# Experts of a routed layer in 12 fixed rounds of four 32-token groups, instead of tiles of 128 rows of one expert each

## The chip, the core and the metric

The kernel runs on one core of a Trainium2 chip. The metric is the device time of one execution in microseconds (us); all inputs and outputs are float32 in HBM. Besides that time there is a profile of one execution, with times from the first to the last instruction of the program (its span). TensorE's matrix work is called PE, its loading of the stationary operand PEld, VectorE DVE, ScalarE ACT, GpSimd POOL, and the engine that issues most transfers SP.

## The reference

One layer of a diffusion backbone for 128 context tokens and 512 latent tokens (640 in all, width 1024): modulation, a projection, attention beside an RWKV-7 scan, an output projection, and then a mixture of experts. Only the last part is touched by the change:

```python
def hier_moe(h, lp):
    x = h.reshape(B * T, D)
    lc = x @ router_c + router_c_b;  g_idx = argmax(lc)                  # 1 of 4 groups
    lf_sel = (x @ router_f + router_f_b) of the chosen group             # 4 experts
    top_w, top_i = lax.top_k(softmax(lf_sel), 2);  top_w /= sum(top_w)   # 2 of 4 experts
    for e in range(16):
        hid = silu(x @ exp_gate[e]) * (x @ exp_up[e])                    # 1024 -> 512
        out = out + combine[:, e:e+1] * (hid @ exp_down[e])              # 512 -> 1024
```

Each of the 640 tokens goes to two experts, so 1280 rows are computed. The weights of one expert are three matrices of 2 MB (gate, up, down). For the inputs that the kernel is run with, the routing of the reference gives the experts 0 to 15 these numbers of rows: 92, 108, 58, 72, 60, 110, 137, 69, 86, 59, 70, 59, 98, 49, 108, 45.

## The kernel before

The program is a row of blocks; at the end of a block all engines wait for each other. The earlier blocks (modulation, projection, attention, scan) take some 570 us and are not changed but for one store and a table of constants. The block from line 1753 on does the output projection, the second norm and the routing. POOL scatters each token's row to the region of its two experts in a scratch tensor in HBM (`xg_d`, 640 rows for each expert; line 1777, two batches, of 3 and of 2 token tiles). DVE counts the rows of each expert and writes a table (lines 2088 to 2106): for each tile of 128 rows its expert and its first row, and how many pairs of tiles there are. An expert with up to 128 rows has one tile, one with 137 has two. The block from line 2143 on works through that table in a loop with a number of turns known only at run time, two tiles to a turn, after a first tile (expert 0) that stands ahead of the loop. For tile i:

- SP loads the weights of the tile's expert into one of two places, `wg`, `wu`, `wd`, with gate and up when the tile before has finished its up product (`u6_mm`) and down when the down product of the tile two before has ended (`y6_mm`). It also loads the tile's 128 token rows (`load_x`).
- PE turns the 128 rows (`x_turn`, 8 turnings of 128x128, line 2178), multiplies them by gate and up (line 2186, 16 products of 128 rows by 512 columns), turns the hidden values (`h_turn`, line 2192) and multiplies by down (line 2200, 8 products). The order in the loop is turn of the hidden values of i-1, gate and up of i, turn of the rows of i+1, down of i-1.
- ACT and DVE take the results out of PSUM (lines 2232 to 2245, 2277 to 2285), and ACT stores the tile's 128 output rows (line 2248) in `yg_d`.

The weights are read as `"(k p) n -> p k n"`: partition p gets the matrix rows p, 128+p, 256+p and so on, in stretches of 2 KB each (gate, up) or 4 KB each (down). PE reads a turning's source as 128 neighbouring columns.

SP has loaded the weights of expert 0 in the block before: up at its start (line 1763), gate when the last tile's concatenation is done (1765), down when the output projection is done (1767). No other expert is known before the table is written.

The last block (line 2305) gathers for each token its two output rows, by indices in `back_i`, weighs and adds them, and stores the outputs.

## Time and profile before

| | us |
|---|---|
| median of 3 runs | 1112.93 |
| lowest and highest run | 1109.16, 1114.7 |
| span of the profiled execution | 1107.9 |
| expert block, first to last PE instruction | 688.7 to 1073.4 |
| one tile of an expert on PE, steady | 21.94 |

The page gives the profiled execution by its span alone; what lies around the span, before the first and after the last instruction, is not shown. The span is 5.0 us under the median of the runs. A line of the trace that shows a group of instructions gives the start of the first, the time from there to the end of the last, the engine, the line of the kernel, and in brackets how long the engine had been idle before and who released it. Each float32 product shows as two MATMUL records.

### The profile page before, as it was taken

What the parts mean: (1) busy time and instruction counts of PE and PEld (TensorE: products, weight loads), DVE (VectorE), ACT (ScalarE), POOL (GpSimd) and SP (SyncE); (2) the same over time, 40 slices, a digit from 0 to 9 for tenths busy, and PEclk for the clock granted to TensorE, in tenths of its full rate; (3) what the DMA queues carried; (4) which work ended last, traced back from release to release, by engine and by line L of the source; (5) the groups of instructions that cost most, each with busy time, mean ns of one, the idle gap of its engine ahead of it and who ended that gap; (6) DMA issues with size and microseconds to landing.
All of it is one profiled execution on the core that took longest, in us unless ns stands there. A gap on an engine that the chain in (4) does not pass through costs nothing. (4 is left out here: it accounts for less than half of the span.)

```text
span 1107.9 us, 18535 instructions
## 1 busy us (share of the span) xinstructions
PE 970.2 (88%) x7858; PEld 575.7 (52%) x7858; DVE 424.7 (38%) x783; ACT 274.8 (25%) x522; POOL 81.4 (7%) x133
## 2 busy tenths in 40 slices
PE   4899999979778778999979982999999999999960
PEld 1465555536456568899954552444444444444420
DVE  2323642233388876687756554000000000000006
ACT  2221222223676622233230120111111111111112
POOL 0600000010000020122200003000000000000002
PEclk9999999998699966999989985999999999999995
DMA  9904342538999510133246226969899899989717
GB/s 332 306 9 152 124 168 89 191 120 352 407 404 403 219 50 8 45 81 96 70 130 243 77 76 247 365 230 333 314 347 346 318 329 347 345 310 337 281 40 282
DMA packets 98629, 247.18 MB, mean 223 GB/s; under 512 B 7540, under 2 KB 12564, under 8 KB 98304
## 3 DMA queue, kind: packets, MB, share of 16 engines
q1 hardware_dynamic: 87104, 219.91, 54.7%
q0 software_dynamic: 5632, 13.97, 4.1%
q10 hardware_dynamic: 5824, 12.28, 2.8%
q8 instruction: 55, 0.90, 0.3%
q14 instruction: 14, 0.11, 0.0%
HBM read 176.51 MB, written 67.01 MB: 220 GB/s over the span
## 5 line engine op out<-in xcount | busy, mean ns | idle before, releaser
L2186 PE MATMUL ps<-arena 128*128 128x512 f32 x544 | 238.9, 596 | 1.7 <-ACT arena L2236 1.7
L2186 PEld LDWEIGHTS ps<-arena 128*128 128x128 f32 x544 | 102.4, 191 | 126.3 <-issue 125.6
L2200 PE MATMUL ps<-arena 128*128 128x512 f32 x272 | 121.2, 598 | 3.6 <-ACT arena L2240 3.6
L711 PE MATMUL ps<-arena 128*128 128x512 f32 (+3 forms) x448 | 123.6, 435 | 0.0
L711 PEld LDWEIGHTS ps<-arena 128*128 128x128 f32 (+1 forms) x448 | 67.7, 188 | 60.2 <-issue 59.3
L2200 PEld LDWEIGHTS ps<-arena 128*128 128x128 f32 x272 | 50.7, 191 | 61.9 <-issue 61.9
L1855 PE MATMUL ps<-arena 128*128 128x512 f32 x160 | 72.4, 606 | 1.9 <-PEq L1324 1.9
L2277 DVE TENSOR_TENSOR arena<-arena,ps 128x512 f32<-128x512 f32 x17 | 11.7, 689 | 136.0 <-ACT arena L2232 136.0
L578 DVE SCALAR_TENSOR_TENSOR arena<-arena 128x128 f32<-128x128 f32 (+3 forms) x56 | 30.9, 552 | 82.6 <-ACT arena L447 81.1
L2285 DVE COPY arena<-ps 128x512 f32<-128x512 f32 x17 | 11.8, 692 | 125.7 <-PE ps L2200 125.7
L644 PE MATMUL ps<-arena 128*128 128x512 f32 (+1 forms) x160 | 52.6, 485 | 1.1 <-ACT arena L405 1.1
L2236 ACT ACTIVATE arena<-ps 128x1024 f32<-128x1024 f32 x18 | 18.5, 1026 | 140.2 <-PE ps L2178 140.2
L1855 PEld LDWEIGHTS ps<-arena 128*128 128x128 f32 x160 | 30.3, 194 | 36.9 <-issue 36.9
L2280 DVE TENSOR_TENSOR arena<-arena,ps 128x512 f32<-128x512 f32 x17 | 11.7, 689 | 94.6 <-PE ps L2186 94.6
L956 PE MATMUL ps<-arena 128*128 128x128 f32 x160 | 26.0, 297 | 22.9 <-DVE arena L1180 19.5
L615 PE MATMUL ps<-arena 128*32 128x512 f32 x192 | 28.6, 635 | 15.7 <-DMA arena<-in_w_mod_dram 15.7
L644 PEld LDWEIGHTS ps<-arena 128*128 128x128 f32 x160 | 29.8, 189 | 20.8 <-issue 17.4
L1366 POOL DMA_DIRECT2D arena<-arena x40 | 20.5, 519 | 258.8 <-issue 155.7
L2310 POOL DMA_INDIRECT arena<-expert_outputs,back_i x10 | 9.8, 984 | 401.0 <-PEq L2305 398.2
L2245 ACT ACTIVATE arena<-ps 128x512 f32<-128x512 f32 x17 | 10.2, 598 | 103.0 <-PE ps L2200 103.0
L1174 DVE TENSOR_REDUCE arena<-ps 128x1 f32<-128x640 f32 x32 | 24.9, 820 | 26.9 <-PE ps L936 26.9
L956 PEld LDWEIGHTS ps<-arena 128*128 128x128 f32 x160 | 18.1, 148 | 29.1 <-DVE arena L1180 23.1
(311 smaller groups left out, 1342.9 us busy)
## 6 DMA issues: line engine op xcount, KB each, us to landing
gathered_tokens<-arena SPq DMA_DIRECT2D x16, 2560.0 KB, 27.0
arena<-in_exp_up_dram SPq DMA_DIRECT2D x17, 2048.0 KB, 18.0
arena<-in_exp_gate_dram SPq DMA_DIRECT2D x17, 2048.0 KB, 13.0
arena<-in_exp_down_dram SPq DMA_DIRECT2D x17, 2048.0 KB, 9.9
arena<-in_w_mod_dram SPq DMA_DIRECT2D x12, 2048.0 KB, 12.4
arena<-gathered_tokens SPq DMA_DIRECT2D x18, 512.0 KB, 15.3
expert_outputs<-arena ACTq DMA_DIRECT2D x17, 512.0 KB, 8.1
arena<-in_w_in_dram SPq DMA_DIRECT2D x4, 2048.0 KB, 8.6
```

What stands on the lines that cost most here:

```text
L578: ins = dve.scalar_tensor_tensor(o[:, a:b], r_[:, base + off:base + off + b - a], mu[0:m, k, e:e + 1], o[:, a:b], ALU.mult, ALU.add)
L615: mm = pe.matmul(ps[32 * g:32 * g + 32, bank, :], cond32[:, k, :], ring[:, slot_of(what), k, :], start=(k < 4), stop=(k >= 4))
L644: mm = pe.matmul(ps[:, b + half, 0:w], hT[:, k, tt * P:(tt + 1) * P], ring[:, slot_of(("qkv", half)), k, 0:w], start=(k == 0), stop=(k == ...
L711: mm = pe.matmul(ps[0:m, b, 0:hi - lo], ring[:, slot_of(what), k, (e % 4) * P:(e % 4) * P + m], hT[:, k, lo:hi], start=(k == 0), stop=(k = ...
L956: mm = pe.transpose(ps[:, 4 + y // 4, (y % 4) * P:(y % 4 + 1) * P], prob[:, g, y * P:(y + 1) * P], ident)
L1174: dve.tensor_reduce(negmax[:, n:n + 1], score_banks(g), AX.X, ALU.max, negate=True).then_inc(max_ok, 1)
L1366: pool.dma_start(rows(u, 1 - z)[:, z, p * NC4:(p + 1) * NC4], rows(vt, p)[:, chunk_at(z, s)]).then_inc(ld_v[s % 2], 16)
L1855: mm = pe.matmul(ps[:, b, :], catT[k4][:, j, tt * P:(tt + 1) * P], wout[:, half, NC4 * k4 + j, :], start=(k4 == 0 and j == 0), stop=(k4 == ...
L2186: mm = pe.matmul(ps[:, b, :], xgT[:, k, :], w[u][:, k, :], start=(k == 0), stop=(k == KT - 1))
L2200: mm = pe.matmul(ps[:, Y0 + half, :], hidT[:, k, :], wd[u][:, k, half * 512:(half + 1) * 512], start=(k == 0), stop=(k == 3))
L2236: act.activation(xgT, ps[:, XT0:XT0 + 2, :].rearrange("p b (k t) -> p (b k) t", t=P), ACT.Copy).then_inc(xgT_ok, 1)
L2285: dve.tensor_copy(yo[:, u, 512:], ps[:, Y0 + 1, :]).then_inc(yo_v, 1)
```

## The change

The experts are taken in a fixed number of 12 rounds, each of 128 columns of tokens in four groups of 32. There are 16 places for experts in a fixed order; place n has a capacity of `CAPQ[n]` groups of 32 rows (48 groups in all), and `RANK_OF[n]` says the expert of which rank in the order of counts stands there (0 for the fullest). Expert 0 always has the first place, of 96 rows. A round can hold the end of one expert's places and the start of the next: five rounds (1, 2, 4, 8, 10) have one expert, four (3, 6, 9, 11) have two experts with 64 rows each, three (0, 5, 7) have two with 96 and 32 rows. In a round with two experts PE makes each product in two pieces of 64 or four pieces of 32 stationary columns, each with the weights of its own expert as the moving operand and its own PSUM partitions. Rows over a place's capacity would go through a loop after the rounds, one tile of 128 at a time; the counts above all fit.

```diff
-NT = 25
-MIN_TILES = NE
+QROWS = 32
+CAPQ = (3, 5, 4, 2, 2, 4, 3, 3, 3, 3, 4, 2, 2, 4, 2, 2)
+RANK_OF = (15, 0, 1, 9, 10, 2, 5, 6, 7, 8, 3, 11, 12, 4, 13, 14)
+NR = sum(CAPQ) // 4
+NOV = 12
...
-        wg = [view(WG0, KT, FE), view(CB, KT, FE)]
...
+        wg = [view(RING + j * PIECE, KT, FE) for j in (8, 7, 6)]
+        wu = [view(RING + j * PIECE, KT, FE) for j in (4, 5, 3)]
+        wd = [view(RING + j * PIECE, 4, D) for j in (1, 2, 0)]
...
+        def gate_of(e):
+            return exp_gate[0][bass.ds(e, 1)].squeeze(0).rearrange("(p k) n -> p k n", p=P)
...
+        def load_rows(eng, r):
+            for n, c0, q0, nq in SEGS[r]:
+                row = row_at(eng, n) if n else 0
+                src = xg_d[bass.ds(row + QROWS * q0, QROWS * nq), :] if n else xg_d[QROWS * q0:QROWS * (q0 + nq), :]
+                eng.dma_start(xg[r % 2][QROWS * c0:QROWS * (c0 + nq)], src).then_inc(ld_xg[r % 2], 16)
...
-                sp.dma_start(wu[0], exp_up[0, 0].rearrange("(k p) n -> p k n", p=P)).then_inc(ld_gu[0], 16)
                 sp.wait_ge(cat_ok, NTT)
...
+                sp.wait_ge(scattered[0], 96)
                 sp.wait_ge(table_ok, 1)
+                for n in (1, 2):
+                    e = expert_at(sp, n)
+                    sp.dma_start(wg[n], gate_of(e)).then_inc(ld_g[n], 16)
+                    sp.dma_start(wu[n], up_of(e)).then_inc(ld_u[n], 16)
+                    if n == 2:
+                        sp.wait_ge(scattered[1], 64)
+                    sp.dma_start(wd[n], down_of(e)).then_inc(ld_d[n], 16)
...
+                act.wait_ge(table_ok, 1)
+                act.wait_ge(scattered[0], 96)
+                act.wait_ge(scattered[1], 64)
+                load_rows(act, 0)
...
+                order = sorted([(LAST_ROUND[n - 3], k, n) for n in range(3, NE) for k in (0, 1)]
+                               + [(LAST_ROUND[n - 3] + 1, 2, n) for n in range(3, NE)])
+                for r, k, n in order:
+                    e = expert_at(sp, n)
+                    if k == 0:
+                        sp.wait_ge(g6_mm, r + 1)
+                        sp.dma_start(wg[n % 3], gate_of(e)).then_inc(ld_g[n % 3], 16)
...
-                        mm = pe.transpose(ps[:, XT0 + k // 4, (k % 4) * P:(k % 4 + 1) * P], xg[:, u, k * P:(k + 1) * P], ident)
+                        mm = pe.transpose(ps[:, XT0 + k // 4, (k % 4) * P:(k % 4 + 1) * P], xg[r % 2][:, k::KT], ident)
...
+                        for k in range(KT):
+                            for c, m, n in tiles_of(r):
+                                mm = pe.matmul(ps[c:c + m, b, :], xgT[:, k, c:c + m], w[n % 3][:, k, :], start=(k == 0), stop=(k == KT - 1))
+                        mm.then_inc(done, 1)
```

There are three places in SBUF for weights instead of two, and the next expert's weights may be loaded as soon as the last round of the expert three before has finished with its matrix. All weights are read as `"(p k) n -> p k n"`: partition p gets 8 (down: 4) neighbouring matrix rows, one stretch of 16 KB. To fit this, a turning reads every eighth column of the token rows, and every fourth of the hidden values (`xg[r % 2][:, k::KT]`, `hid[:, k::4]`); it is the stationary operand that is stepped. The token rows are loaded by ACT, the output rows go through one buffer instead of two, and the table that SP waits for is shorter (an order of 16 experts). The overflow table, the indices for the gather and part of the weighing are computed by DVE between its work of rounds 0 to 2. One store of zeros, in an earlier block, grows from 9 to 12 blocks of 128 rows (4608 to 6144 KB).

What stands on SP in a row, from the end of the projection block on; before, with the loads of expert 0 (lines 1763 to 1767), the end of the block (1753) and the first two loads of token rows (2157, 2154); the loop with its loads of weights comes behind them:

```order
L1763 DMA arena<-in_exp_up_dram 128x8x512
L1765 DMA arena<-in_exp_gate_dram 128x8x512
L1767 DMA arena<-in_exp_down_dram 128x4x1024
L1753 UNCONDITIONAL_BRANCH
L2144 UNCONDITIONAL_BRANCH
L2137 TENSOR_LOAD eid_i
L2137 ISA x2
L2157 DMA arena<-gathered_tokens 128x1024
L2141 TENSOR_LOAD row_i
L2141 ISA x2
L2154 ISA
L2154 DMA arena<-gathered_tokens 128x1024
```

And now, where lines 1812 to 1816 load expert 0, and lines 1744 to 1827 read the number of the expert in place 1 from the table and load it:

```order
L1812 DMA arena<-in_exp_gate_dram 128x4096
L1814 DMA arena<-in_exp_up_dram 128x4096
L1816 DMA arena<-in_exp_down_dram 128x4096
L1744 TENSOR_LOAD plan_i
L1744 ISA x2
L1823 ISA
L1823 DMA arena<-in_exp_gate_dram 128x4096
L1824 DMA arena<-in_exp_up_dram 128x4096
L1827 DMA arena<-in_exp_down_dram 128x4096
```

The last six rows stand once more, for place 2, and only then comes the branch at the end of the block (line 1753, now 1801): the loads of places 1 and 2 have moved ahead of it, the loads of token rows have left SP, and every load of weights is one stretch of 4096 numbers for each partition.

What stands on PE in a row at the start of the expert block; before, as far as the loop's first turning of rows (line 2178 turns rows, 2186 is gate and up, 2192 turns the hidden values):

```order
L2178 MATMUL ps<-arena 128x128 x8
L2186 MATMUL ps<-arena 128x512 x16
L2178 MATMUL ps<-arena 128x128 x8
L2210 UNCONDITIONAL_BRANCH
L2211 COMPARE_AND_BRANCH
L2190 ISA
L2192 MATMUL ps<-arena 128x128 x4
L2182 ISA
L2183 REGISTER_ALU
L2186 MATMUL ps<-arena 128x512 x16
L2176 ISA
L2178 MATMUL ps<-arena 128x128 x8
```

And now, from the first product on, where line 2221 turns rows, 2232 is gate and up, 2238 turns the hidden values and 2252 is down; the gate and up products of rounds 0, 1, 2 and 3 stand here, in pieces of 32, 128, 128 and 64 rows:

```order
L2232 MATMUL ps<-arena 32x512 x64
L2221 MATMUL ps<-arena 128x128 x8
L2238 MATMUL ps<-arena 128x128 x4
L2232 MATMUL ps<-arena 128x512 x16
L2221 MATMUL ps<-arena 128x128 x8
L2252 MATMUL ps<-arena 32x512 x32
L2238 MATMUL ps<-arena 128x128 x4
L2232 MATMUL ps<-arena 128x512 x16
L2221 MATMUL ps<-arena 128x128 x8
L2252 MATMUL ps<-arena 128x512 x8
L2238 MATMUL ps<-arena 128x128 x4
L2232 MATMUL ps<-arena 64x512 x32
```

The order of turnings and products from one round to the next is that of the loop; only the products of seven of the twelve rounds are cut into two or four pieces, each piece as wide (512) as the whole one was.

## Rows read from the trace of the kernel before

**Rows 1.** The page, part 2: busy tenths in 40 slices of the span.
```profile
PE   4899999979778778999979982999999999999960
DMA  9904342538999510133246226969899899989717
```
**Rows 2.** The page, part 5 (groups by line, the two costliest matmul lines).
```profile
L2186 PE MATMUL ps<-arena 128*128 128x512 f32 x544 | 238.9, 596 | 1.7 <-ACT arena L2236 1.7
L2200 PE MATMUL ps<-arena 128*128 128x512 f32 x272 | 121.2, 598 | 3.6 <-ACT arena L2240 3.6
```
**Rows 3.** Instructions in order of time on PE, one tile in the middle.
```profile
1017.13 13.93 PE L2186 MATMUL ps<-arena 128*128 128x512 f32 x32
1030.89 1.03 PE L2178 MATMUL ps<-arena 128*128 128x128 f32 x8
1031.77 7.03 PE L2200 MATMUL ps<-arena 128*128 128x512 f32 x16
1038.64 0.60 PE L2192 MATMUL ps<-arena 128*128 128x128 f32 x4
1039.07 13.93 PE L2186 MATMUL ps<-arena 128*128 128x512 f32 x32
```
**Rows 4.** Windows: busy time of PE, PEld, DVE, ACT, POOL; clock, DMA share, GB/s.
```profile
841.58:863.53 21.95, 21.95 (x63) 10.29 (x62) 1.98 (x4) 2.75 (x5) 0.00 (x0) 1.00 0.91 334
```
**Rows 5.** Instructions in order of time, from the table to the first product.
```profile
679.03 0.95 POOL L1777 DMA_INDIRECT gathered_tokens<-arena,slot_i  x1 [0.30 <-issue]
680.19 0.15 DVE L2106 CAST eid_i<-arena 128x1 int32<-128x1 f32 x1
...
685.11 0.34 SPq L2157 DMA_DIRECT2D arena<-gathered_tokens  x1
686.25 0.36 SPq L2154 DMA_DIRECT2D arena<-gathered_tokens  x1
688.38 0.38 SPq L2147 DMA_DIRECT2D arena<-in_exp_gate_dram  x1
...
688.72 1.97 PE L2178 MATMUL ps<-arena 128*128 128x128 f32 x8 [15.21 <-DMA arena<-gathered_tokens]
...
691.89 15.95 PE L2186 MATMUL ps<-arena 128*128 128x512 f32 x32 [1.21 <-ACT arena L2236]
```
**Rows 6.** Instructions in order of time, end of the expert block.
```profile
1064.05 0.60 ACT L2240 ACTIVATE arena<-ps 128x512 f32<-128x512 f32 x1 [2.67 <-issue]
1064.79 8.63 PE L2200 MATMUL ps<-arena 128*128 128x512 f32 x16 [3.61 <-ACT arena L2240]
```
**Rows 7.** Instructions in order of time on PE: products in pieces of 32 columns.
```profile
18.15 1.93 PE L615 MATMUL ps<-arena 128*32 128x512 f32 x16 [1.68 <-DMA arena<-in_w_mod_dram]
20.00 3.70 PE L624 MATMUL ps<-arena 128*128 128x512 f32 x8
```
**Rows 8.** One line's instructions (ns min/median/max), where the moving operand is stepped, and one where not.
```profile
L1402 PE MATMUL ps<-arena x640: 210/228/258, 419.7 to 550.1; 32*32 32x32 f32 x160
L1451 PE MATMUL ps<-arena x640: 211/213/311, 427.6 to 562.5; 32*32 32x64 f32 x160
```
**Rows 9.** Groups by line and form, 715 to 1070 us: stationary loads of the turnings.
```profile
L2178 PEld LDWEIGHTS ps<-arena 128*128 128x128 f32 x128 | 14.9, 141 | 8.5 <-issue 8.5
```
**Rows 10.** Windows, columns as in rows 4: stretches with the transfer engines full.
```profile
10.00:20.00 10.00, 5.49 (x32) 1.09 (x32) 0.68 (x1) 0.60 (x1) 0.00 (x0) 1.00 1.03 382
320.00:340.00 20.00, 15.03 (x141) 11.25 (x139) 17.17 (x34) 14.52 (x36) 0.00 (x0) 1.00 1.03 403
```
**Rows 11.** Waits of SP's queue: line waited at, for whom, us in total, times, longest.
```profile
SPq L842 <- DMA expert_outputs<-arena: 25.6, 1, 25.6
SPq L842 <- PEq L842: 29.1, 1, 29.1
```

**Rows 12.** The page, part 6: transfers by line, KB each, us to landing.
```profile
arena<-in_exp_gate_dram SPq DMA_DIRECT2D x17, 2048.0 KB, 13.0
arena<-gathered_tokens SPq DMA_DIRECT2D x18, 512.0 KB, 15.3
```

More of the change, by code:

```diff
@@ L106, in const_table @@
     put("prio", np.broadcast_to(np.array([4, 3, 2, 1]), (P, 4)))
-    put("tile_iota", np.broadcast_to(np.arange(NT + 1), (P, NT + 1)))
+    put("tile_iota", np.broadcast_to(np.arange(NE), (P, NE)))
     put("expert_row", np.broadcast_to(np.arange(NE) * T, (P, NE)))
+    put("tie", np.broadcast_to(np.where(np.arange(NE) == 0, -20000, NE - 1 - np.arange(NE)), (P, NE)))
+    put("rank_of", np.broadcast_to(np.array(RANK_OF), (P, NE)))
+    place = np.argsort(np.array(RANK_OF))
+    cap = QROWS * np.array(CAPQ)
+    put("cap_rows", np.broadcast_to(cap[place], (P, NE)))
+    put("out_row", np.broadcast_to((np.cumsum(cap) - cap)[place], (P, NE)))
     return out
@@ new lines, in expert_at, with row_at @@
+        def expert_at(eng, n):
+            return eng.value_load(plan_i[0:1, n:n + 1], min_val=0, max_val=NE - 1)
+        def row_at(eng, n):
+            return eng.value_load(plan_i[0:1, NE + n:NE + n + 1], min_val=0, max_val=(NE - 1) * T)
+        xg = [view(P, D), view(CB + D, D)]
+        SEGS = [[] for _ in range(NR)]
+        FIRST_ROUND, LAST_ROUND = [], []
+        for n in range(NE):
+            at, to = sum(CAPQ[:n]), sum(CAPQ[:n + 1])
+            FIRST_ROUND.append(at // 4)
+            LAST_ROUND.append((to - 1) // 4)
+            for r in range(at // 4, (to - 1) // 4 + 1):
+                lo, hi = max(at, 4 * r), min(to, 4 * r + 4)
+                SEGS[r].append((n, lo - 4 * r, lo - at, hi - lo))
@@ L1722, in build, with rows_landed @@
+        def load_rows(eng, r):
[3 more added lines that the diff above has]
+                eng.dma_start(xg[r % 2][QROWS * c0:QROWS * (c0 + nq)], src).then_inc(ld_xg[r % 2], 16)
+        def rows_landed(r):
+            return 16 * sum(len(SEGS[i]) for i in range(r % 2, r + 1, 2))
         lv = [LORA_AT]
@@ L2222, in _ @@
-                last = pe.snap(pairs * 2)
-                h_turn(last)
-                pe.wait_ge(yo_a, last + 1)
-                pe.wait_ge(yo_v, last + 1)
-                down(last, 0, pairs * 16 + 16)
+                x_turn(0)
+                gate_up(0)
+                x_turn(1)
+                h_turn(0)
+                for r in range(1, NR):
+                    gate_up(r)
+                    if r + 1 < NR:
+                        x_turn(r + 1)
+                    down(r - 1)
+                    h_turn(r)
@@ L2254, in _ @@
+                load_rows(act, 1)
                 x_out(0)
@@ new lines, in _ @@
+                hidden(0)
+                hot = overflow_table()
+                for r in range(1, NR):
+                    hidden(r)
+                    if r == 1:
+                        overflow_rows(hot)
+                    if r == 2:
+                        result_rows()
+                        weigh(3, NTT)
+                    y_out(r - 1)
+                y_out(NR - 1)
+                dve.wait_ge(over_ok, 1)
+                more = n_over(dve)
+                with dve.If(more > 0):
+                    with dve.Fori(0, NOV) as j:
+                        with dve.If(j < more):
+                            dve.wait_ge(o_sg, j + 1)
+                            dve.tensor_tensor(sg, sg, ps[:, GA, :], ALU.mult).then_inc(o_hs, 1)
+                            dve.wait_ge(o_hs, j + 1)
+                            dve.wait_ge(o_um, j + 2)
+                            dve.tensor_tensor(hid, sg, ps[:, UP, :], ALU.mult).then_inc(o_hid, 1)
+                            dve.wait_ge(o_ym, j + 2)
+                            dve.tensor_copy(yo[:, 512:], ps[:, Y0 + 1, :]).then_inc(o_yv, 1)
```

412 lines of the change are left out of this document (247 added, 165 removed).

## The prediction

> **What bounds the kernel now.** I read the page first. The slices show PE full in the last two fifths of the span, from slice 26 on, and the transfer engines at eight or nine tenths over the same stretch [rows 1]; so two things are nearly full there, and the question is which one sets the pace. By line, the two groups of products of the experts are 238.9 and 121.2 us of PE, and they wait for almost nothing, 1.7 and 3.6 us in all [rows 2]. In order of time one tile runs without a gap: gate and up from 1017.13, the next rows' turnings at 1030.89, down at 1031.77, the hidden values' turnings at 1038.64, and the next tile's gate at 1039.07, 21.94 us after the last one [rows 3]. The window of another tile has PE busy in all of its 21.95 us at full clock, the transfers at 0.91 of their time and 334 GB/s, and DVE and ACT with 2 to 3 us each [rows 4]. So PE sets the pace of the 17 tiles and the transfers keep up with a tenth to spare. The reader is to see that 17 x 128 rows are computed for 1280 rows that are wanted: 41% of PE's work is padding.
>
> **The tiles that go.** The routing gives 15 experts with up to 128 rows and one with 137: 17 tiles, and the trace has 17 loads of gate weights [rows 12]. The places' capacities in the order of ranks take all counts: the fullest expert, 137 rows, has 160; the tightest is 60 rows in 64. So nothing goes through the loop behind the rounds, and 12 rounds stand for 17 tiles: 5 x 21.94 = 109.7 us less, if a round costs a tile. The order on PE within a round is that of the loop, so the covers stay the same ones: ACT and DVE take out gate and up while the next turnings and the down product run, and the small DVE work that moves into rounds 0 to 2, at most some 20 operations of a fifth to a third of a microsecond in a round, has 20 us of idle DVE to lie in [rows 4].
>
> **Rounds in pieces.** Three rounds have four pieces of 32 columns and four rounds two pieces of 64. Down of one whole tile is 8 products in 1038.64 - 1031.77 = 6.87 us, 0.86 each [rows 3], and each is two records, 0.43 apiece. If pieces ran one behind the other, a round of four pieces would need 72 more products (61.8 us) and one of two pieces 24 more (20.6 us): 3 x 61.8 + 4 x 20.6 = 268 us. The modulation at the start of this kernel already does products in four pieces of 32, with a different moving operand for each: 16 records in 1.93 us [rows 7], where 16 x 0.43 would be 6.9. Four run side by side, in 4 x 0.43 = 1.72 us plus one pass's latency. The next product, with the whole array, starts at 20.00, before the pieces' modelled end at 20.08, so the change between shapes costs nothing that is seen. Seven rounds have four such changes each; at 0 to 0.3 us that is 0 to 8 us. I take 2.
>
> The Trainium skill, page "TensorE: Matmul & The Clock Gate", Part 3, has a lower figure: three column pieces with 512 moving columns measured 2.38 times as fast as one by one, 0.79 of full. No row here shows that loss; by it the three rounds of four pieces would be 20.6 x (1/0.79 - 1) = 5.5 us longer each and the sum some 16 us higher by them alone, as an estimate from that page. The trace's 1.93 us decides for me.
>
> **Stepped turnings.** Each round has 8 turnings of rows and 4 of hidden values, 144 in all, whose stationary operand is now read in steps of 8 or 4 numbers. No stationary operand of the trace is stepped like this. A contiguous one loads in 141 ns [rows 9], under the product before it, and 8 turnings take 1.03 us [rows 3], 0.13 each. The nearest row is a moving operand in steps of 32 numbers: 32 of them take 228 ns in the median where 64 contiguous ones take 213 [rows 8]. This excludes little more than a slowdown to double per number. At double, a load is 0.28 us and no longer hidden: 0.15 x 144 = 22 us. Below zero there is nothing, since a stepped read reads no less. The minima, 210 against 211 ns, speak for none; I take 0 and keep 22 for the range.
>
> The Trainium skill, page "SBUF — State Buffer", section "Door 1: The DMA port swizzle", states that SBUF has lines of 16 bytes and that each access to a new line pays a penalty, so float32 may step less than four numbers for free. Both steps here change the line with each number. It gives no size; by it, as I read it, the sum would stand towards the 22 us. It is the second rival below.
>
> **Weights.** Now 15 experts of 6.29 MB are loaded after the table, 94.4 MB, with 12 loads of rows and 12 stores of 0.52 MB each: 107 MB. The engines give 382 GB/s when they are full with stretches of 2 KB, and 403 with 4 KB rows [rows 10]; the window of a tile, 334 GB/s at a share of 0.91, would be 367 at full [rows 4]. For stretches of 16 KB there is no row; the two above rise with the stretch. From the table at about 678 (next term), the last byte is there at 678 + 107000/B: 942 at 403, 958 at 382, 970 at 367. PE needs the last down weights at about 960 (below). So the price is 0 to 12 us, and a little where a place in SBUF comes free late at 382; I take 2. The transfers cease to be a reserve of a tenth and become a near tie.
>
> **The start.** The table is done at 680.19 now [rows 5]. Its replacement is 8 or 9 short operations instead of 17, so it is ready some 2 us earlier, at 678, and the loads of two experts start at once, instead of at 688.38 behind the block's end. The rows of round 0 do not gain: they wait for the last scatter (issued at 679.03 [rows 5]), and the scatter and they now share the transfer engines with 12 MB of weights. The last 1.5 MB of the scatter and the 0.5 MB of rows at half of 390 GB/s cost 4 and 1.3 us more; ACT reads the row number in about 1.1 us, as SP does between 685.11 and 686.25. Without the block's end between scatter and load, some 2 us come back. First turning at 688.72 + 3; gate of round 0 at 691.89 + 3 = 694.9. Bounds: -2 (all hidden) to +10 (two experts' whole gate and up first). I take +3.
>
> **The end.** From the first gate to the last down product are 1064.79 - 691.89 = 372.9 us, less 109.7 is 263.2; the last down begins at 694.9 + 263.2 + 2 = 960. The wait of 3.61 us before it, 2.67 of which was ACT leaving the loop [rows 6], shrinks by about 2; reading the overflow number and the branch behind the last store add about 1.1 and a bit. I take 0, with -2 to +3. The gather and the sums, 30 us after it, are unchanged. The larger store of zeros is 1.57 MB, 4 us at 403 GB/s; SP's waits at the end of that block are 25.6 us for the transfers and then 29.1 us for PE [rows 11], so 4 us vanish in the 29.1.
>
> **The sum.** 1107.9 - 109.7 (tiles) + 2 (pieces) + 0 (steps) + 2 (transfers) + 3 (start) + 0 (end) = 1005.2 us of span. The median of the runs is 5.0 above the profiled span: 1010 us.
>
> **Rivals.**
> 1. Transfers set the pace. For it: 107 MB in some 280 us, and a share that is at 0.91 today. Against it: the rates of rows 10, and longer stretches. If the engines gave only 350 GB/s, the last weights would come at 984, 24 us after PE wants them: 1032 us. The DMA line would show nines throughout and PE would wait for exp weights in most rounds.
> 2. Stepped turnings cost double or more: 1010 + 22 = 1032, or less in part, since a slower PE also hides the transfers' 2 us.
> 3. The other side, slower than before: the pieces of different experts don't run side by side, since each has its own moving operand in another place of SBUF and its own wait. Fully in a row they cost 268 us: 1278 us. It decides from 103/268, that is when 38% of the overlap is lost. Against it: rows 7 have four different moving operands too.
> 4. The change doesn't do what it says: rows run over a place's capacity. Each such tile is 6.29 MB loaded with nothing beside it (16 us at 390 GB/s) and 22 us of PE at half the clock at first, some 45 us; one gives 1055, three would eat the gain. The counts speak against it.
>
> **How the numbers follow.** The forecast, with its own range of 1001 to 1019, has 0.66; rival 1 has 0.14, rival 2 0.14, rival 3 0.03, rival 4 0.01, and 0.02 is left for what I don't see. The range of 80% goes from 1001 (start and end at their low bounds, no price for transfers and pieces: 1107.9 - 109.7 - 2 - 2 + 5.0 = 999, of which not all will come together) to 1034, where rivals 1 and 2 stand. The measurement can tell about 0.5%, 5.6 us, from no change. Faster than that: all but rivals 3 and part of 4, 0.95; within it 0.01; slower 0.04.
>
> **What would show it right or wrong.** Rounds in the profile after: gate to gate 21.9 us, alike for 128, 64 and 32 columns; if rounds 0, 5, 7 are longer than 1 and 2, the pieces cost, and if all are longer by the same, the turnings do (8 in 1.03 us now). PEld of the turnings at 141 ns. Waits of PE for weights under 5 us in all, GB/s near 400 in the windows. First gate near 695, last down begun near 960, span near 1005. The forecast is wrong if a round takes over 23.5 us or if the engines with 16 KB stretches stay under 370 GB/s.

## The result and the profile after

| | before | changed | forecast |
|---|---|---|---|
| median, us | 1112.65 | 1049.34 | 1010 |
| lowest and highest | 1109.16, 1114.7 | 1045.91, 1054.08 | 1001 to 1034 (80%) |
| ratio to before | | 0.9444 [0.9405, 0.9483] | |
| span of the profiled execution | 1107.9 | 1049.7 | 1005.2 |
| last scatter issued | 679.03 | 682.18 | 679.03 |
| first turning of rows | 688.72 | 700.66 | 691.7 |
| first gate product | 691.89 | 703.74 | 694.9 |
| last down product begins | 1064.79 | 1007.95 | 960 |

The change is faster by 63 us where 103 were forecast; the time lies above the range. The page of the changed kernel, the busy tenths of PE, its granted clock and the transfers in 40 slices of 26.2 us, beside [rows 1]:

```profile
PE   3799999997977776899997999429997889798960
PEclk9899999998879997699998999659999989989995
DMA  9911525443999962013322720899899879979417
```

The slices 28 to 38 should all be nines for PE. They are sevens to nines, so PE waits within the rounds. The waits of PE from 690 us on, one line for each line waited at: for whom, us in all, times, longest:

```profile
PE ps L2221 <- DMA arena<-gathered_tokens: 51.0, 6, 23.9
PE ps L2232 <- ACT arena L2310: 1.7, 2, 1.1
PE ps L2252 <- ACT arena L2314: 1.5, 1, 1.5
```

There is no wait for an expert's weights. Nearly all of PE's waiting is for the token rows of a round: 23.9 us ahead of the first round, and 27.1 us in five waits within the rounds (of 6.20, 7.68, 6.57, 4.38 and 2.27 us, ahead of the turnings of rounds 5, 6, 9, 10 and 11). PE in order of time around two of the waits, and behind them two rounds without one, to be laid beside [rows 3] (line 2232 is gate and up, 2221 the turning of rows, 2252 down, 2238 the turning of hidden values):

```profile
789.38 13.90 PE L2232 MATMUL ps<-arena 128*128 128x512 f32 x32
809.48 1.97 PE L2221 MATMUL ps<-arena 128*128 128x128 f32 x8 [6.20 <-DMA arena<-gathered_tokens]
...
820.98 13.94 PE L2232 MATMUL ps<-arena 128*32 128x512 f32 x128
842.60 1.97 PE L2221 MATMUL ps<-arena 128*128 128x128 f32 x8 [7.68 <-DMA arena<-gathered_tokens]
...
852.60 13.95 PE L2232 MATMUL ps<-arena 128*64 128x512 f32 x64
866.49 1.16 PE L2221 MATMUL ps<-arena 128*128 128x128 f32 x8
867.57 7.07 PE L2252 MATMUL ps<-arena 128*32 128x512 f32 x64
874.58 0.75 PE L2238 MATMUL ps<-arena 128*128 128x128 f32 x4
875.26 13.94 PE L2232 MATMUL ps<-arena 128*32 128x512 f32 x128
```

The round from 852.60 takes 22.66 us to the next gate, and the gate and up products take 13.90 us whole, 13.95 in two pieces and 13.94 in four. So rounds are close to what the forecast said they would be, wherever the rows are there. Behind the four longer waits the turnings take 1.97 us instead of 1.16. The windows say why (columns as in [rows 4], the clock before the last two numbers): a stretch ahead of the first wait within the rounds, one behind it, the first 3.5 us of that one alone, and last the wait itself:

```profile
789.38:803.00 13.62, 13.62 (x34) 5.90 (x32) 1.11 (x2) 1.53 (x3) 0.00 (x0) 1.00 1.01 402
809.48:821.00 11.52, 11.52 (x47) 4.79 (x47) 0.58 (x1) 1.60 (x2) 0.00 (x0) 0.75 0.60 252
809.48:813.00 3.52, 3.52 (x12) 2.10 (x14) 0.00 (x0) 1.02 (x1) 0.00 (x0) 0.50 1.01 428
```
```profile
803.00:809.00 6.00, 0.28 (x1) 0.00 (x0) 0.69 (x1) 0.00 (x0) 0.00 (x0) 0.95 1.04 343
```

While PE stands still the transfer engines are full, at 343 GB/s. When it goes on, the granted clock averages 0.75: in the first 3.5 us it is 0.50, the lower of the two levels, 1.2 GHz. That is dear: a round's down products, 7.03 to 7.13 us at full clock, take 9.00, 7.84, 9.19, 7.89 and 8.78 us behind the five waits. Once PE is behind, SP's next loads, which wait for PE's products, are behind too (none is issued between 803.46 and 820.56), and the share falls to 0.60.

What SP and ACT issue ahead of the first of these waits (SPq and ACTq: the issue of a transfer; line 2323 is the store of output rows, 1764 the load of rows):

```profile
789.25 0.34 SPq L2198 DMA_DIRECT2D arena<-in_exp_down_dram  x1
789.89 0.34 ACTq L2323 DMA_DIRECT2D expert_outputs<-arena  x1
790.95 1.40 ACTq L1764 DMA_DIRECT2D arena<-gathered_tokens  x2
```

The rows that PE wants when gate and up are done, at 803.3, are asked for at 790.95. That is 12 us ahead, behind the store of 512 KB in the same queue and beside the weights. Between 720 and 985 us the transfers took to landing (KB each, median us; compare [rows 12]):

```profile
expert_outputs<-arena ACTq DMA_DIRECT2D x9, 512.0 KB, 10.3
arena<-gathered_tokens ACTq DMA_DIRECT2D x8, 256.0 KB, 14.0
arena<-gathered_tokens ACTq DMA_DIRECT2D x2, 384.0 KB, 13.2
```

The third kind of load, five of 512 KB for the rounds with one expert, took 10.0. Before, a load of rows took 15.3 us too, behind two loads of weights in SP's own queue, but the one issued from 779.35 to 787.46 had landed at 797.50 and was turned only at 811.46. Now the rows have some 12 us. From asking to the landing of a round's last rows it took 9.6 to 10.9 us in five of rounds 2 to 11, and 13.4 to 19.1 us in the five that PE waited for. What the transfer engines did in 792 to 800 us, by queue (q1 is SP's, q10 ACT's: packets, MB, share of the engines' time):

```profile
q1 hardware_dynamic: 194, 2.74, 83.8%
q10 hardware_dynamic: 143, 0.54, 16.4%
```

2.74 MB in packets of 16 KB are 167, and the trace has 131 packets of 4 KB beside them (the other 12 of ACT's queue are small). In this window the weights take 84% of the time and the rows and the store 16%. One packet of 16 KB took 0.61 us (median of 6144) and one of 4 KB 0.16. Store and rows of a round are 256 packets of 4 KB, 16 for each of the 16 engines; if each waits for one packet of weights they take 16 x 0.77 = 12.3 us, as an estimate, and more if packets take longer than their median.

The packets of the whole trace bear this out, and say which rounds it strikes. In rounds 5, 6, 9 and 10 the 256 packets of store and rows stand beside 257 to 284 packets of weights, 1.00 to 1.11 for each, and the stretch from the first to the last of them is 12.7 to 16.0 us. In rounds 3, 4, 7 and 8, which had no wait, only 74 to 98 packets of weights stand beside the 256, and the stretch is 6.1 to 7.9 us: SP's queue had run dry on the way, and for 1.2 to 1.7 us no packet of weights starts on any engine, which never happens in the stretches of rounds 5, 6, 9 and 10. Round 11, with the shortest wait, lies between, 165 packets and 11.6 us. Ahead of round 5 SP had asked for 10 MB within 15 us (774.44 to 789.59), ahead of round 4 for 6 MB (752.31 to 767.28), since the places of two experts that end in one round are asked for again together. One packet of weights for one of rows, while there are weights to move, is the theory that the experiments had to test against others.

### The profile page after: what moved, and what is told of

Same layout as the page of the kernel before. It is cut to its first block and busy times, and to the rows that moved or that the text cites. A ratio compares the mean times of both kernels' runs of the same rounds, so it can differ in the third digit from the quotient of the medians.

```text
span 1049.7 us, 18864 instructions
## 1 busy us (share of the span) xinstructions
PE 876.3 (83%) x8174; PEld 510.4 (49%) x8174; DVE 421.5 (40%) x795; ACT 259.4 (25%) x502; POOL 81.1 (8%) x133
## 5 line engine op out<-in xcount | busy, mean ns | idle before, releaser
L2232 PE MATMUL ps<-arena 128*32 128x512 f32 (+2 forms) x800 | 170.0, 609 | 1.7 <-ACT arena L2310 1.7
L2232 PEld LDWEIGHTS ps<-arena 128*32 128x32 f32 (+2 forms) x800 | 60.5, 137 | 102.7 <-issue 99.7
L2252 PE MATMUL ps<-arena 128*32 128x512 f32 (+2 forms) x400 | 92.2, 641 | 1.5 <-ACT arena L2314 1.5
L1916 PE MATMUL ps<-arena 128*128 128x512 f32 x160 | 72.2, 605 | 1.9 <-PEq L1334 1.9
L2221 PE MATMUL ps<-arena 128*128 128x128 f32 x96 | 17.8, 343 | 51.0 <-DMA arena<-gathered_tokens 51.0
L2252 PEld LDWEIGHTS ps<-arena 128*32 128x32 f32 (+2 forms) x400 | 31.9, 145 | 54.2 <-issue 53.8
L654 PE MATMUL ps<-arena 128*128 128x512 f32 (+1 forms) x160 | 55.4, 506 | 1.1 <-ACT arena L415 1.1
L2445 DVE COPY arena<-ps 128x512 f32<-128x512 f32 x12 | 8.3, 692 | 116.7 <-PE ps L2252 116.7
L2436 DVE TENSOR_TENSOR arena<-arena,ps 128x512 f32<-128x512 f32 x12 | 8.2, 687 | 112.5 <-ACT arena L2306 112.5
L1916 PEld LDWEIGHTS ps<-arena 128*128 128x128 f32 x160 | 30.3, 194 | 36.7 <-issue 36.7
L2310 ACT ACTIVATE arena<-ps 128x1024 f32<-128x1024 f32 x12 | 12.3, 1024 | 138.3 <-PE ps L2221 138.3
L966 PE MATMUL ps<-arena 128*128 128x128 f32 x160 | 25.3, 291 | 23.9 <-DVE arena L1190 20.5
L2221 PEld LDWEIGHTS ps<-arena 128*128 128x128 f32 x96 | 14.7, 204 | 59.7 <-DMA arena<-gathered_tokens 55.9
L654 PEld LDWEIGHTS ps<-arena 128*128 128x128 f32 x160 | 31.1, 197 | 22.4 <-issue 19.0
L2439 DVE TENSOR_TENSOR arena<-arena,ps 128x512 f32<-128x512 f32 x12 | 8.3, 688 | 67.4 <-PE ps L2232 67.4
## 6 DMA issues: line engine op xcount, KB each, us to landing
arena<-in_exp_gate_dram SPq DMA_DIRECT2D x16, 2048.0 KB, 12.7
arena<-in_w_mod_dram SPq DMA_DIRECT2D x12, 2048.0 KB, 12.7
```

The costliest lines, as they stand in the source:

```text
L654: mm = pe.matmul(ps[:, b + half, 0:w], hT[:, k, tt * P:(tt + 1) * P], ring[:, slot_of(("qkv", half)), k, 0:w], start=(k == 0), stop=(k == ...
L966: mm = pe.transpose(ps[:, 4 + y // 4, (y % 4) * P:(y % 4 + 1) * P], prob[:, g, y * P:(y + 1) * P], ident)
L1916: mm = pe.matmul(ps[:, b, :], catT[k4][:, j, tt * P:(tt + 1) * P], wout[:, half, NC4 * k4 + j, :], start=(k4 == 0 and j == 0), stop=(k4 == ...
L2221: mm = pe.transpose(ps[:, XT0 + k // 4, (k % 4) * P:(k % 4 + 1) * P], xg[r % 2][:, k::KT], ident)
L2232: mm = pe.matmul(ps[c:c + m, b, :], xgT[:, k, c:c + m], w[n % 3][:, k, :], start=(k == 0), stop=(k == KT - 1))
L2252: mm = pe.matmul(ps[c:c + m, Y0 + half, :], hidT[:, k, c:c + m], wd[n % 3][:, k, half * 512:(half + 1) * 512], start=(k == 0), stop=(k == 3))
```

## The experiments

The theories stand in the expectations as they were named ahead of the runs. A is that the rows take turns with 16 KB packets of weights. B means two things: in e1 to e3 that the transfer engines are simply full, in f2 (and so in f1) that the store ahead of the rows in their queue delays them. C, in g1, is A and the second B together, and D that the moment of asking decides. The profiled executions differ by how late the last scatter was issued, from 677.4 to 687.2 us in the seven kernels whose instructions ahead of it are the same (changed, e1, e3, e4, f2, f3, g1), and at 675.5 in g3. So this table counts from there: last scatter to first turning, first gate to last down product, and PE's waits for transfers within the rounds (us).

| run | start | rounds | waits | median | ratio to before |
|---|---|---|---|---|---|
| changed kernel | 18.5 | 304.2 | 27.1 | 1049.3 | 0.9444 |
| e1 rows early | 18.8 | 264.3 | 0 | 1012.3 | 0.9121 |
| e2 short stretches | 27.3 | 265.2 | 0.8 | 1023.9 | 0.9208 |
| e3 late start | 18.7 | 304.3 | 27.6 | 1047.7 | 0.943 |
| e4 no steps | 18.8 | 305.7 | 31.1 | 1058.5 (one run) | |
| f1 4 KB packets | 24.6 | 264.9 | 0 | 1016.3 | 0.9143 |
| f2 store by GpSimd | 23.3 | 269.4 | 4.2 | 1021.6 | 0.9185 |
| f3 rows early, late start | 18.6 | 264.7 | 0 | 1013.5 | 0.911 |
| f4 short, late start | 15.5 | 268.0 | 2.6 | 1009.5 | 0.9075 |
| g1 rows before store | 23.5 | 270.4 | 3.2 | 1021.3 | 0.9154 |
| g2 short, late, rows early | 15.2 | 268.4 | 2.2 | 1011.0 | 0.9071 |
| g3 4 KB, late, rows early | 15.5 | 264.1 | 0 | 1006.2 | 0.9054 |
| forecast | 12.7 | 265.1 | | 1010 | |

**e1.** The rows are asked for earlier in ACT's order: those of round 5 at 754.92, 28.8 us ahead of round 4's gate product (783.70), where the changed kernel asks 1.6 us behind it.

```diff
                 load_rows(act, 1)
                 x_out(0)
+                load_rows(act, 2)
                 sigmoid(0)
                 x_out(1)
+                load_rows(act, 3)
...
-                    if r + 1 < NR:
-                        load_rows(act, r + 1)
                     sigmoid(r)
                     if r + 1 < NR:
                         x_out(r + 1)
+                    if r + 3 < NR:
+                        load_rows(act, r + 3)
```

> One edit to the changed kernel: ACT issues the rows of round r+2 as soon as the turning of round r is known to be done, some 22 us earlier than now. Theory A (the rows come late because they stand behind a store in ACT's queue and share each transfer engine, packet by packet, with weights in 16 KB packets): the 27.1 us in which PE waits for rows and some 11 us of half clock behind these waits go, weights are still never waited for, span about 1049.7 - 38 = 1012 us. Theory B (the transfer engines are simply full, and whatever comes first something else comes late): PE then waits for weights instead, and the gain is under 10 us.

1012.3 us, 0.9121 [0.9065, 0.9176]. The only wait for rows is the first, and the rounds take 264.3 us, 39.9 less than in the changed kernel. Of that 27.1 are the waits, 10.6 the lower clock in turnings and down products behind them, and 1.3 a shorter first gate and up (15.46 us for 16.75), at which the edit did not aim. The window of a round of four pieces, columns as above, has PE busy throughout at full clock beside 386 GB/s, where the changed kernel had 343 GB/s and a still PE:

```profile
800.00:822.00 22.00, 22.00 (x169) 7.73 (x166) 2.06 (x3) 2.61 (x4) 0.00 (x0) 1.00 1.01 386
```

So the wait for the rows and what hangs on it is the whole loss within the rounds but for some 1 to 2 us. The engines had the time to bring everything: full engines alone (theory B here) would have made PE wait for weights instead, and it never does.

**e2.** The old layout of the weights, `"(k p) n -> p k n"`, stretches of 2 and 4 KB, and turnings without steps.

```diff
-            return exp_gate[0][bass.ds(e, 1)].squeeze(0).rearrange("(p k) n -> p k n", p=P)
+            return exp_gate[0][bass.ds(e, 1)].squeeze(0).rearrange("(k p) n -> p k n", p=P)
...
-                        mm = pe.transpose(ps[:, XT0 + k // 4, (k % 4) * P:(k % 4 + 1) * P], xg[r % 2][:, k::KT], ident)
+                        mm = pe.transpose(ps[:, XT0 + k // 4, (k % 4) * P:(k % 4 + 1) * P], xg[r % 2][:, k * P:(k + 1) * P], ident)
```

> One edit to the changed kernel: the weights are read as in the kernel before, in stretches of 2 KB (gate, up) and 4 KB (down), and the turnings are not stepped. Theory A (share of packets): 512 KB of rows land in 8 to 12 us instead of 12.9 in the median, so most of the 27.1 us of waits for rows go although the engines' full rate falls from some 425 to 382 GB/s; span 1015 to 1030 us. Theory B (engines full): the lower rate makes the waits longer, span 1050 to 1065 us.

1023.9 us, 0.9208 [0.9136, 0.9279]. The rows are asked for as late as in the changed kernel, and are never waited for: they land in 7.3 us instead of 14.0. The only wait within the rounds is one of 0.8 us for up weights.

```profile
arena<-gathered_tokens ACTq DMA_DIRECT2D x8, 256.0 KB, 7.3
```

The rounds are as short as in e1. The start is 27.3 us: the block's end waits until SP has issued the many short stretches of two experts. This changes two things at once, so it could not say whether the packets or the layout did it.

**e3.** Only gate and up of place 1 are asked for in the block before; the rest when the rows of round 0 have landed.

```diff
-                for n in (1, 2):
-                    e = expert_at(sp, n)
-                    sp.dma_start(wg[n], gate_of(e)).then_inc(ld_g[n], 16)
...
+                e = expert_at(sp, 1)
+                sp.dma_start(wg[1], gate_of(e)).then_inc(ld_g[1], 16)
+                sp.dma_start(wu[1], up_of(e)).then_inc(ld_u[1], 16)
...
+                sp.wait_ge(ld_xg[0], rows_landed(0))
+                e = expert_at(sp, 1)
+                sp.dma_start(wd[1], down_of(e)).then_inc(ld_d[1], 16)
```

> One edit to the changed kernel: of the 12 MB of weights that SP issues ahead of the end of the projection block only gate and up of place 1 stay there; the rest is issued once the rows of round 0 have landed. Theory A: the rows of round 0 land about 5 MB of traffic earlier, first gate at about 696 instead of 703.7 us, span about 7 us less, 1043 us, the waits for rows in the later rounds unchanged. Theory B (engines full): what is gained at the start comes back as a wait for the weights of place 1 or 2 in rounds 0 to 2, span unchanged.

1047.7 us, 0.943 [0.9354, 0.9505]: no difference to the changed kernel, and the start is 18.7 us against 18.5. My expectation missed: 8 MB less beside the rows do not bring the first round forward. The trace shows the 4 MB of gate and up that are left being moved until the rows are there: up lands at 698.65, the rows are turned at 697.92.

**e4.** Turnings without steps, weights still in 16 KB stretches. The columns of the token rows then do not belong to the rows of the weights, so this kernel computes other numbers in the expert layer; its instructions and transfers are the same.

```diff
-                        mm = pe.transpose(ps[:, HT, k * P:(k + 1) * P], hid[:, k::4], ident)
+                        mm = pe.transpose(ps[:, HT, k * P:(k + 1) * P], hid[:, k * P:(k + 1) * P], ident)
```

> One edit to the changed kernel: the turnings read neighbouring columns; the weights are still read in 16 KB stretches, so rows of weights and of tokens no longer belong together and the outputs are other numbers. If stepping costs PE time, a round without a wait is shorter than the 22.06 to 22.66 us of the changed kernel, by up to 1.8 us; if it only lengthens the hidden loading of the stationary operand (204 ns in the mean now, 141 before), loads go back to 141 ns and the rounds keep their length within 0.2 us.

One run, 1058.5 us, with the latest scatter of all and 31.1 us of waits; its time decides nothing. What it tells is in the loads of the turnings' stationary operand from 850 to 906 us, first e4, then the changed kernel (count, busy us, mean ns; compare [rows 9]):

```profile
L2221 PEld LDWEIGHTS ps<-arena 128*128 128x128 f32 x16 | 1.7, 141 | 3.6 <-DMA arena<-gathered_tokens 2.8 <-issue 0.8
```
```profile
L2221 PEld LDWEIGHTS ps<-arena 128*128 128x128 f32 x16 | 1.9, 194 | 1.6 <-issue 1.6
```

Steps of eight numbers make a load longer by 53 ns, 38%; the loads of the hidden values, in steps of four, take 207 ns in the same stretch where e4 has 140. But eight turnings take 1.16 us instead of 1.09 in rounds of pieces, and four of the hidden values 0.75 instead of 0.66: 0.16 us in such a round, less in a whole one, under 2 us in all, as the second half of the expectation had it.

**f1.** The layout stays, each load of weights is made in four transfers of 4 KB for each partition.

```diff
+        def in_four(eng, dst, src, done):
+            k = dst.shape[1] // 4
+            for j in range(4):
+                eng.dma_start(dst[:, j * k:(j + 1) * k, :], src[:, j * k:(j + 1) * k, :]).then_inc(done, 16)
...
-                        sp.dma_start(wg[n % 3], gate_of(e)).then_inc(ld_g[n % 3], 16)
+                        in_four(sp, wg[n % 3], gate_of(e), ld_g[n % 3])
```

> Every load of weights is made in four transfers of 4 KB for each partition, with the same layout in SBUF; nothing else differs from the changed kernel. Theory A (the rows' packets of 4 KB take turns with packets of 16 KB, so their transfer is slowed by the size of the other queue's packets): the rows land in 7 to 8 us (median) instead of 12.9, PE's waits for rows in rounds 1 to 11 fall from 27.1 us to under 5, about 1049 - 27 - 10 = 1012 us, plus what the start loses if SP issues more transfers there (up to 10 us). Theory B (they are late because they stand behind the output store, whatever the packets are): waits as before, 27 us, and 1049 us.

1016.3 us, 0.9143 [0.9061, 0.9224], no wait for rows within the rounds:

```profile
expert_outputs<-arena ACTq DMA_DIRECT2D x12, 512.0 KB, 6.9
arena<-gathered_tokens ACTq DMA_DIRECT2D x8, 256.0 KB, 8.4
```

The same bytes, in the same order and layout, asked for at the same places; only the packets of the other queue are shorter. By one for one, store and rows should take 16 x (0.16 + 0.16) = 5.1 us in place of 12.3, beside what a transfer takes at least (2.7 us for a store with nothing beside it, at 1006.75 in the changed kernel). In rounds 3 to 11 their packets stretch over 5.9 to 6.8 us, with 0.96 to 1.44 packets of weights for each. The start loses to SP's issuing, as in e2. Theory A holds.

**f2.** The store goes through GpSimd's queue.

```diff
-                    act.dma_start(yg_d[r * P:(r + 1) * P, :], yo).then_inc(y_st, 16)
...
+            @block.gpsimd
+            def _(pool):
+                for r in range(NR):
+                    pool.wait_ge(yo_a, r + 1)
+                    pool.wait_ge(yo_v, r + 1)
+                    pool.dma_start(yg_d[r * P:(r + 1) * P, :], yo).then_inc(y_st, 16)
```

> The store of a round's output rows is issued by GpSimd instead of ScalarE; the rows are still asked for at the same place in ScalarE's order, with 16 KB stretches of weights beside them. Theory B (the store ahead of them in the same queue makes the rows late): the rows land some 4 to 6 us earlier, most of the 27.1 us of waits and the half clock behind them go, about 1015 us. Theory A (turns with 16 KB packets, store or no store): the store's packets now take turns too, the rows land as late as before or later, waits 20 to 35 us, 1042 to 1060 us.

1021.6 us, 0.9185 [0.9118, 0.9253]; waits in the rounds 4.2 us in four, the rows land in 10.6 us with 16 KB packets beside them. So theory B, as put against A, holds too: A and B were not rivals. Shorter packets alone take the waits away, and the store out of the queue alone takes all but 4.2 us.

**g1.** The only edit: the rows of round r+3 are asked for directly ahead of the store of round r.

```diff
                     act.wait_ge(yo_v, r + 1)
+                    if r + 3 < NR:
+                        load_rows(act, r + 3)
                     act.dma_start(yg_d[r * P:(r + 1) * P, :], yo).then_inc(y_st, 16)
...
-                    if r + 1 < NR:
+                    if r == 1:
                         load_rows(act, r + 1)
```

> The rows of round r+3 are asked for by ScalarE directly ahead of the store of round r instead of directly behind it: the same engine, the same queue, the same moment within some 1 us; weights in 16 KB packets as in the changed kernel. Theory C (both together: a queue gets one 4 KB packet for each 16 KB packet of weights, some 0.77 us a turn on each transfer engine; the rows alone are 8 turns, 6.2 us, store and rows together 16 turns, 12.4 us): the rows land in 8 to 9 us (median) instead of 12.9, the waits of 27.1 us in rounds 1 to 11 fall under 3, about 1013 us; the store then takes 11 to 13 us, which nobody waits for. Theory A alone (packet size, store or no store ahead): landing and waits hardly change, 1040 to 1050 us. Theory D (it is the moment of asking, and only an earlier one helps): waits as before.

1021.3 us, 0.9154 [0.9088, 0.922]; waits of 3.2 us in three, where 27.1 were. Same engine, queue and packets, and the request at the same moment within 1 us. The landing times change places:

```profile
expert_outputs<-arena ACTq DMA_DIRECT2D x11, 512.0 KB, 16.5
arena<-gathered_tokens ACTq DMA_DIRECT2D x8, 256.0 KB, 9.8
```

Theory C, which has both, gave 8 to 9 us for the rows, 11 to 13 for the store, waits under 3 us and 1013 us. It has the direction right, and is short by 1 us for the rows, by 4 us for the store and by 8 us for the time, half of which is the start. D falls, since the moment hardly moved; A alone falls too.

In f2 and g1 the start is 23.3 and 23.5 us instead of 18.5 to 18.8: there ACT asks for the rows of round 0 only 10.3 us after the last scatter, for whose landing it waits, instead of 5.6, and they then take another 13. Nothing that these two kernels change lies ahead of it. What makes this difference stays open; it accounts for about half of their distance to e1.

**f3, f4, g2, g3**, put together from the edits above.

> Rows asked for two rounds ahead, and of places 1 and 2 only gate and up of place 1 asked for before the rows of round 0 have landed. If the two gains add: 1012.3 - 2 = 1010 us, first gate near 697 to 701. If the weights kept back are then late for rounds 1 and 2 (the down of place 1, the gate of place 2), PE waits there for weights by 3 to 8 us and the time is 1013 to 1020.

1013.5 us, 0.911 [0.9048, 0.9171]; rows early is the whole gain, and the late start again brings nothing beside 16 KB packets (18.6 us). No wait for weights.

> Weights in stretches of 2 and 4 KB, unstepped turnings, and the late start of places 1 and 2 of the kernel before this one; rows asked for as in the changed kernel. If the short stretches alone lose only by the block's end, which waited for SP's issuing of transfers (first gate 711.6): first gate near 700, no waits for rows, rounds of 22.1, so about 1023.9 - 11 = 1013 us. If short stretches also feed the rounds too slowly: waits for weights in the rounds, 1018 to 1025.

1009.5 us, 0.9075 [0.9005, 0.9145]. With short packets the late start does count: 15.5 us, against 27.3 in e2, and 18.7 in e3 with its 16 KB packets. One wait for up weights of 2.6 us near the end of the rounds:

```profile
946.41 8.54 PE L2235 MATMUL ps<-arena 128*64 128x512 f32 x32 [2.60 <-DMA arena<-in_exp_up_dram]
```

> Short stretches, unstepped turnings, late start of places 1 and 2, rows two rounds ahead. The rows were already on time with short stretches, so asking earlier brings nothing there: first gate near 696, rounds of 22.1, and 1009 us; if the third load of rows at the start meets the weights of place 1, first gate 1 to 3 us later, 1011 us.

1011.0 us, 0.9071 [0.9035, 0.9106], as expected no gain over f4. The same single wait for up, 2.2 us: stretches of 2 KB feed the rounds only just.

> Weights in 4 KB stretches of the 16 KB layout (stepped turnings), late start of places 1 and 2, rows two rounds ahead. Against f1 (1016.3 us) the block's end no longer waits for SP's issuing: first gate near 697 instead of 707, so 1007 us. If SP's issuing of 24 transfers (about 15 us) behind the rows makes the weights of places 1 and 2 late: waits for weights of 2 to 6 us in rounds 0 to 2, 1010 to 1013 us.

1006.2 us, 0.9054 [0.9009, 0.9099], the lowest median of all, though its interval overlaps with those of e1, f1, f3, f4, g1 and g2, so that none of these is shown to be the fastest. It beats the kernel before by 9.5% and the changed kernel by some 4%. Its first product comes at 694.12, the last down at 958.24, and nothing is waited for between them but ACT:

```profile
691.04 1.97 PE L2229 MATMUL ps<-arena 128*128 128x128 f32 x8 [20.91 <-DMA arena<-gathered_tokens]
694.12 15.26 PE L2240 MATMUL ps<-arena 128*32 128x512 f32 x128 [1.11 <-ACT arena L2318]
...
958.24 7.09 PE L2260 MATMUL ps<-arena 128*64 128x512 f32 x32 [1.54 <-ACT arena L2322]
```

In a round it moves 401 GB/s (800 to 822 us) with packets of 4 KB on both queues.

## Why the prediction was wrong

**The step that failed is the term "Weights", +2 us.** It counted bytes against a rate, 107 MB at about 390 GB/s, and asked when the last of them would be there. In total that was right: the weights were never waited for, and the engines gave 402 GB/s where they were full ahead of the first wait (343 in it). But a round waits for each transfer, and its rows are the last asked for and behind a store in their own queue, beside a queue whose packets are four times as large. I wrote that "the covers stay the same ones", and looked for the covers of ACT's and DVE's work alone; I did not follow how far ahead of their use the rows of a round are asked for. The rows of before gave a warning: 15.3 us to landing [rows 12], if behind weights in their own queue, where the changed kernel asks 12 us ahead. In place of 2 us this cost 27.1 us of waits and some 11 of lower clock behind them, 38 us. Rival 1 had the right resource and the wrong shape: it wanted PE to wait for weights in most rounds, and PE never does; rates under 370 GB/s are there only in stretches where rows and store go beside the weights (343, above).

The Trainium skill, page "DMA: Bandwidth & Descriptors", section "Queues, rings and completion order", states that each transfer engine goes round the queues that have work, one packet from each in turn. The trace agrees in the ratio: 1.00 to 1.11 packets of 16 KB for each of 4 KB in rounds 5, 6, 9 and 10, and f1, where shorter packets alone bring the landing from 14.0 to 8.4 us. The section has a packet of several descriptors, and what the trace counts as a packet here is one stretch of 16 or 4 KB; that these are the same thing is not shown. By that rule stretches of 16 KB delay the rows beside them, and this would have been the rival that I lacked.

**The start, +3, measured +11.9.** Of that, 3.15 us are that the last scatter came later, which varies by 9.7 us between the profiled executions of kernels that are the same up to there. From the scatter to the first turning it was 18.5 us instead of 9.7 before and 12.7 forecast. Counted from the forecast, the first gate product came 8.8 us late (703.74 for 694.9). That the whole +11.9 lies above the bound of +10 is the late scatter, which is bad luck; without it the start is +8.8 (11.9 less 3.15), within the bounds of -2 to +10, and far from the value taken. The rows were asked for 5.6 us after the last scatter, about as before (6.1), so the slower scatter that I had priced at 4 us did not show. But their landing took 12.9 us where it had taken 3.6: I shared the engines by bytes, half for the rows; by packets of 16 and 4 KB they get a fifth, and between 687.76 and 700.6 ACT's queue moved 0.61 MB beside 4.08 MB of weights.

**Right.** The tiles: 12 rounds, nothing in the overflow, and 264.3 us from first gate to last down in e1 against 265.1 forecast. The pieces: 13.94 and 13.95 us against 13.90 whole, so they run wholly side by side and rival 3 falls; the lower figure for column pieces that I cited from the Trainium skill, page "TensorE: Matmul & The Clock Gate", Part 3, is not what this kernel shows. With the turnings' 0.1 to 0.2 us, rounds without a wait took 22.1 to 22.7 us, and my 2 us for pieces was about right. The steps: 194 ns and not 141, where rival 2 asked for double, and hidden but for under 2 us, so rival 2 falls; the penalty of which the Trainium skill, page "SBUF — State Buffer", section "Door 1: The DMA port swizzle", speaks shows here in the load and hardly in the time. The end: 41.73 us from the last down's start to the end of the span, 43.13 before. The larger store of zeros vanished as said; SP waits 29.2 us for it and then still 24.2 for PE, where it had waited 25.6 and 29.1 [rows 11]. Two slips in the working change nothing: at 403 GB/s the last weights would be there at 943.5 and not at 942, and in one of the slices that I called eight or nine tenths full the transfer engines were at six [rows 1].

**The sum again.** 1005.2 + 8.8 (start) + 39.0 (rounds: 27.1 of waits, 10.6 of lower clock behind them, 0.8 of a first gate and up longer than before, 0.5 left over) - 1.4 (end) - 2 (transfers, which the rounds now hold) = 1049.6 us of span; 1049.7 were measured.

## What to carry to other kernels

In this kernel a small and urgent transfer was priced by its queue, not by its bytes. To price one, count the packets ahead of it in its own queue, give each the time of one packet of the other busy queues beside its own, add what a transfer takes alone, and compare with how long ahead of its use it is asked for. Ask too when the other queue is full and when it runs dry: here the same kind of load landed in 10 or in 19 us by that. Put the load before the store when both go through one queue, and ask one buffer earlier if there is one. Longer stretches raised the rate of the weights, and cost more than they gave as long as the rows were asked for late (1049.3 us against 1016.3); with the rows asked for early the two are within each other's noise (f3 and g3), and packets of 4 KB were as fast as the work needed.

## What the runs showed of the hardware

- While both had work, two queues shared the transfer engines about one packet for one (1.00 to 1.11 of 16 KB for each of 4 KB in four rounds; 0.96 to 1.44 with 4 KB on both). The same 256 KB of rows landed in a median of 14.0 us behind a store and beside packets of 16 KB, in 9.8 with the store behind them, and in 8.4 behind a store but beside packets of 4 KB.
- A stretch of 16 KB shows as one packet, of 0.61 us in the median; with the engines full they moved up to 436 GB/s in a slice of 9 us, and 401 in a window of 22 us with packets of 4 KB only.
- After waits of 4.4 to 7.7 us PE came back at the lower clock level: eight turnings in 1.97 instead of 1.16 us. After the wait of 2.27 us the turnings took 1.16, and the clock was lower only in the down products behind them (8.78 us instead of 7.09). The five waits, 27.1 us, cost 10.6 us more in this way.
- A stationary operand read in steps of 8 numbers of float32 loads in 194 ns instead of 141, in steps of 4 in 207 instead of 140.
- Four products in pieces of 32 columns, each with a moving operand of another expert, run fully side by side (13.94 us for a round's gate and up, 13.90 whole).
- SP took 0.35 to 0.74 us to issue a load of 2 MB in 16 KB stretches ahead of the block's end, 1.9 to 6.1 us for one in four parts (f1) and 0.4 to 11.3 us for one in stretches of 2 or 4 KB (e2), the long ones behind other loads. There it held up all engines: counted from the last scatter, the first turning came 6 (f1) and 9 us (e2) later.
